# Experts in an order that interleaves the four groups, and the final norm formed inside each expert block

## The reference, cut to what matters

```python
g = jnp.argmax(gl, axis=-1)                       # one group for each token
top_v, top_i = lax.top_k(el_g, 2)                 # two experts inside it
gate = jax.nn.softmax(top_v, axis=-1) * p_g[:, None]
h_e = silu(x @ w_gate[e]) * (x @ w_up[e])         # x: the rows of hn sent to expert e
y = h + sum over the two experts of gate * (h_e @ w_down[e])
y_prompt, y_sample = rmsnorm(y, g_final)          # y / sqrt(mean(y*y) + 1e-6) * g_final
```

## Time and profile before

| | us |
|---|---|
| median of three runs | 2008.78 |
| profiled execution | 2014.13 |
| its span, first to last instruction | 2012.40 |
| TensorE busy in the span | 1877.3 (93%) |
| VectorE, ScalarE, GpSimd busy | 974.0, 773.4, 280.8 |

### The profile page before, as it was taken

The page is one execution under the profiler, slowest core; times in us unless marked ns, Lnnn a source line. Parts: engine busy times, 40 slices in busy tenths (PEclk is TensorE's granted clock), DMA queues, the critical chain, the costliest instruction groups (busy, mean ns, idle before and its releaser), DMA issues. The chain is left out here.

```text
span 2012.4 us, 28492 instructions
## 1 busy us (share of the span) xinstructions
PE 1877.3 (93%) x10232; PEld 1609.9 (80%) x10233; DVE 974.0 (48%) x1929; ACT 773.4 (38%) x1442; POOL 280.8 (14%) x387
## 2 busy tenths in 40 slices
PE   7899999999999999999999937999999999999980
PEld 5899987788888788887888736888888888888870
DVE  5634343546444654445454334445565554646424
ACT  4332323333333333333333204444465444636423
POOL 2000000000201001000010022222222222222223
PEclk9799999999999999999999958999999999999995
DMA  6222233423236222342232517655567566556438
GB/s 220 88 83 84 84 128 119 138 86 102 85 126 209 84 85 96 135 138 93 84 105 87 198 47 230 186 183 184 177 215 257 152 230 188 183 182 228 130 56 343
DMA packets 153429, 293.12 MB, mean 146 GB/s; under 512 B 9341, under 2 KB 75901, under 8 KB 153354
## 3 DMA queue, kind: packets, MB, share of 16 engines
q1 hardware_dynamic: 135930, 232.13, 32.9%
q0 software_dynamic: 15072, 51.45, 10.4%
q10 hardware_dynamic: 2352, 8.52, 1.0%
HBM read 243.02 MB, written 49.07 MB: 145 GB/s over the span
## 5 line engine op out<-in xcount | busy, mean ns | idle before, releaser
L62 PE MATMUL bank<-xT_hi,wh 128*128 128x512 f32 (+1 forms) x960 | 341.0, 355 | 7.2 <-ACT S L745 5.4
L63 PE MATMUL bank<-xT_lo,wh 128*128 128x512 f32 (+1 forms) x960 | 340.4, 355 | 0.0
L64 PE MATMUL bank<-xT_hi,wl 128*128 128x512 f32 (+1 forms) x960 | 339.2, 353 | 0.0
L793 DVE TENSOR_TENSOR wl<-raw,wh 128x512 fp32r<-128x512 f32 x352 | 219.4, 686 | 202.5 <-ACT wh L596 202.4
L1665 PE MATMUL bank<-gu_hi,ex_hi 128*128 128x256 f32 (+1 forms) x960 | 311.6, 325 | 4.6 <-DVE gu_lo L1575 4.6
L1667 PE MATMUL bank<-gu_hi,ex_lo 128*128 128x256 f32 (+1 forms) x960 | 307.3, 320 | 0.0
L1666 PE MATMUL bank<-gu_lo,ex_hi 128*128 128x256 f32 (+1 forms) x960 | 307.3, 320 | 0.0
L596 ACT ACTIVATE wh<-raw 128x512 fp32r<-128x512 f32 x352 | 192.0, 619 | 85.1 <-PE bank L1216 54.7
L62 PEld LDWEIGHTS bank<-xT_hi,wh 128*128 128x128 f32 x960 | 182.3, 190 | 35.9 <-issue 9.7
L1665 PEld LDWEIGHTS bank<-gu_hi,ex_hi 128*128 128x128 f32 x960 | 183.5, 191 | 24.7 <-DVE gu_lo L1575 8.2
L64 PEld LDWEIGHTS bank<-xT_hi,wl 128*128 128x128 f32 x960 | 182.4, 190 | 25.3
(11 more groups left out here) (228 smaller groups left out, 3154.8 us busy)
## 6 DMA issues: line engine op xcount, KB each, us to landing
raw<-in_w_in SPq DMA_DIRECT2D x56, 1024.0 KB, 5.2
raw_gate_up<-in_w_gate SPq DMA_DIRECT2D x16, 2048.0 KB, 8.4
raw_gate_up<-in_w_up SPq DMA_DIRECT2D x16, 2048.0 KB, 13.5
raw_d<-in_w_down SPq DMA_DIRECT2D x16, 2048.0 KB, 12.8
raw<-in_w_out SPq DMA_DIRECT2D x16, 1024.0 KB, 6.3
raw<-in_w_up_pool SPq DMA_DIRECT2D x16, 512.0 KB, 3.5
raw<-in_w_up_gmlp SPq DMA_DIRECT2D x16, 512.0 KB, 4.5
h<-in_x_prompt SPq DMA_DIRECT2D x16, 512.0 KB, 5.0
```

The costliest lines, as they stand in the source:

```text
L62: nc.tensor.matmul(out, lh, rh, start=(i == 0), stop=False)
L63: nc.tensor.matmul(out, lh, rl, start=False, stop=False)
L64: last = nc.tensor.matmul(out, ll, rh, start=False, stop=(i == n - 1))
L793: lo = lambda out, x, hi: tt(out, x, hi.bitcast(F32), ALU.subtract)
```

## The change

`phase_four` goes. Its work moves into the expert blocks. The experts are taken in the order (expert 0 of each of the four groups, then expert 1 of each, ...), so that two experts that can hold the same token never stand next to each other. Weights, slots and block numbers are looked up in that order by nested loops.

Each block now ends in `z`, the block's rows of `h` plus the weighted result. VectorE forms it (`add`, two instructions out of the PSUM banks, in place of ScalarE's `weigh`): at the start of the next block, or inside its weight split where that block is a first one. `z` is written to `h_rows` by a plain scatter. Its norm is formed at once: `square` on ScalarE, `mean` on VectorE, `root` on GpSimd, `scale` on VectorE as the last instruction of the block after the one that made the result. The normed rows are scattered to both outputs at every block: to the prompt output with out-of-range rows dropped, and to the sample output by a third index field that is out of range for every row that isn't a sample row. A token's rows are so written twice, and the later expert's value stays. The rows of `h` for a block are gathered a block ahead (`next_h`).

GpSimd's order for each block is now `step`:

```diff
-def fetch_and_add(col, j): ... gather x; wait y_out; wait y_read; scatter-add to h
+def step(col, j):
+    wait_apart(pool, x_tr, j, passed_pool)
+    nc.gpsimd.tensor_copy(idx_1[:, :], idx[:, :]).then_inc(moved, 1)
+    wait_apart(pool, moved, j, passed_pool)
+    rows_of_x(col, j)
+    store_z(j)
+    next_h(j + 1)
+    root(j)
+    store_final(j)
+    wait_apart(pool, z_out, 16 * j, passed_pool)
+    wait_apart(pool, prompt_out, 16 * j, passed_pool)
+    wait_apart(pool, sample_out, 16 * j, passed_pool)
```

```diff
+def store_final(n):
+    wait_apart(pool, final_ok, n + 1, passed_pool)
+    for to, field, last, landed in ((v["y_prompt"], 0, SEQ - 1, prompt_out),
+                                    (v["y_sample"], 2, SAMPLE - 1, sample_out)):
+        nc.gpsimd.indirect_dma_start(
+            out=to[0], in_=final[:, :], in_offset=None, bounds_check=last, oob_is_err=False,
+            out_offset=bass.IndirectOffsetOnAxis(ap=idx_y[:, field:field + 1], axis=0))\
+            .then_inc(landed, 16)
```

```diff
+def add(n):
+    dve.wait_ge(y_done, n)
+    dve.wait_ge(final_ok, n)
+    dve.wait_ge(h_rows_in, 16 * n)
+    for c in range(2):
+        stt(z[:, cols], bankY[c][:, :], idx_h[:, 1:2].bitcast(F32), h_rows[:, cols], ALU.mult, ALU.add).then_inc(z_ok, 1)
+def scale(n):
+    dve.wait_ge(z_rs, n)
+    dve.wait_ge(moved_y, n)
+    stt(final[:, :], z[:, :], rsz[:, 0:1], v["gf"][:, :], ALU.mult, ALU.mult).then_inc(final_ok, 1)
 def split(i, lo):
     for k in range(2 * KD):
+        if k == KD + 4:
+            add(lo + 1)
 def per_block(e, i, lo, j, first=False):
+    if not first:
+        add(j + 1)
+        mean(j + 1)
     ...
+    if first:
+        mean(j + 1)
     ...
+    scale(j + 1)
-def weigh(j): two ACTIVATE out of bankY
+def square(n):
+    act.wait_ge(z_ok, 2 * n)
+    nc.scalar.activation(sq[:, :], z[:, :], ACT.Square, accum_out=ssz[:, 0:1]).then_inc(z_ss, 1)
```

More of the change, by code:

```diff
@@ L46 @@
 NEG = -3.0e38
+FIELDS = 3
+NOWHERE = 1 << 20
 NPAN = 22
@@ L1032, in place @@
                     for c in range(2):
-                        nc.vector.tensor_copy(pay[0:r, c, span, 0:1].rearrange("p t o -> p (t o)"),
-                                              tok_all[0:r, column:column + span.stop - span.start])
+                        for field, table in ((0, tok_all), (2, sample_all)):
+                            nc.vector.tensor_copy(pay[0:r, c, span, field:field + 1].rearrange("p t o -> p (t o)"),
+                                                  table[0:r, column:column + span.stop - span.start])
                     nc.vector.tensor_copy(weight[:, 0, :], parts[0:r, 0, span])
@@ L1517, in rows_high, with split, per_block @@
                             .then_inc(ex_hi, 1)
[L1518 to L1528, removed]
+                rows_high(1)
+                def square(n):
+                    act.wait_ge(z_ok, 2 * n)
+                    nc.scalar.activation(sq[:, :], z[:, :], ACT.Square, accum_out=ssz[:, 0:1]).then_inc(z_ss, 1)
+                def split(i, lo):
                     use_sigmoid_table(1)
                     act.wait_ge(gu_done, lo + 1)
-                    act.wait_ge(gate_in, 16 * e + 16)
+                    act.wait_ge(gate_in, 16 * i + 16)
                     for k in range(1, 2 * KD):
                         if k == KD:
-                            act.wait_ge(up_in, 16 * e + 16)
-                        if k == KD + 6:
-                            weigh(lo)
+                            act.wait_ge(up_in, 16 * i + 16)
                         nc.scalar.activation(gu[0][:, k, :], raw_gu[:, k, :], ACT.Copy).then_inc(e_hi, 1)
-                def per_block(e, lo, j, first=False):
+                    square(lo + 1)
+                def per_block(e, i, lo, j, first=False):
                     def down(k):
@@ L1548, in per_block @@
                         use_sigmoid_table(0)
-                        weigh(j)
+                        square(j + 1)
                     act.wait_ge(g_done, j + 1)
@@ L1564, in per_block @@
                     if first:
-                        rows_high(j + 3, j)
+                        rows_high(j + 2)
                 experts(act, split, per_block, peel=True)
                 total = act.value_load(blk_tab[0:1, 2 * NE - 1:2 * NE], min_val=1, max_val=MAXBLK)
-                weigh(total)
+                square(total + 1)
             @block.vector
@@ L1647, in per_block @@
                         rows_low(2 * j + 3)
+                    scale(j + 1)
                 experts(dve, split, per_block, peel=True)
+                total = dve.value_load(blk_tab[0:1, 2 * NE - 1:2 * NE], min_val=1, max_val=MAXBLK)
+                add(total + 1)
+                mean(total + 1)
+                scale(total + 1)
             @block.tensor
```

269 lines of the change are left out of this document (123 added, 146 removed).

## The result

| | before | after | predicted |
|---|---|---|---|
| median, us | 2007.47 (2006.15 to 2011.86, 4 runs) | 2146.44 (2139.07 to 2151.68, 4 runs) | 2045 (2000 to 2110) |
| ratio to before | | 1.0685 [1.0652, 1.0718] | 1.018 |
| profiled execution, and its span | 2014.13, 2012.4 | 2151.68, 2149.8 | 2050.4 |

The direction was right, and the loss nearly four times too small. The time went to the expert blocks. First the windows of the changed kernel (stretch; us, PE, PEld, DVE, ACT, POOL busy, granted clock, DMA share, GB/s): the expert blocks, then a loop into a first block, the first 5 us behind it, and the rest of the loop out of that block.

A forecast was written before the change was run, and what follows sets the result against it. Bounds: TensorE's 18.35 us pace in the expert blocks, and the DMA-bound last stage. Loop losses of 84.7 us less gains of 48.4 gave +36.3, or 2050.4 profiled, carried to a median of 2045 us; range 2000 to 2110.

The forecast's parts named there:

- Into a first block: Loop from transposes to transposes ending at an expert's first block: 19.8 us against 18.1 before, late by 1.7, 15 times.
- scaling's end: VectorE's scaling of the normed rows ends 4.8 us after the transposes, or 8.0 after those of a first block.
- landing with the wake: Two stores of normed rows land in 4.9 us on idle DMA engines, 6.4 beside weight loads, before GpSimd goes on.
- from the copy to the gather's issue: On GpSimd after the stores land: wake, two index copies and the gather's issue, 1.7 us together.
- the gather: Fetch of the next block's x rows: 7.5 us into a first block, 5.2 out of one, 4.6 between others.
- this very rule: VectorE instructions with two SBUF inputs block GpSimd: up to 0.4 us per instruction, 30 us more, kept only in the range.
- Out of a first block: Loop starting at an expert's first block: 22.2 us against 18.5 before, late by 3.7, 16 times.
- Between others: Loops between blocks that are not first ones: 16.9 us, under the pace of 18.35, so no loss.
- The gains: Removed last stage saves 45.5 us and an earlier first gather 2.9 us, together 48.4.
- Dear stores: Rival: normed-row stores cost as much as the scatter-add, or the second costs like a full one; 2156 us; chance 0.22.
- Rows in time: Rival: x rows arrive in time and the last stage's gain stays; loss under 3.0 us per expert; 1993 us; chance 0.18.
- VectorE setting the pace: Rival: VectorE's added work in first blocks, not the rows, sets the pace; 52 us lost, 2013 us; chance 0.10.

The follow-up runs named there:

- the run without the hold: Changed kernel with VectorE's low-half split of gate and up weights reading PSUM and one SBUF tensor instead of two SBUF tensors; 2092.67 us, ratio 1.0427.
- the best version: Changed kernel with the gather of the next x rows behind the issue of the normed-row stores but ahead of the wait for their landing; 1984.12 us, ratio 0.9868.

## Why the prediction was wrong

**Into a first block** it failed, by 77 of the 99 us that the loops lost beyond the 84.7 predicted: 15 x (24.98 - 18.13) = 103 us in place of 25. Term by term, in the loop from 1270.26:

- scaling's end 4.72 (predicted 4.8), store's issue 0.91 (0.8), landing with the wake 4.49 (4.9): right;
- **from the copy to the gather's issue 4.79 (1.7 with the wake): the term that was mis-sized.** It was read off, from a place where VectorE was not splitting (the price beside a split stood in the same trace, below);
- the gather 10.71 (7.5): 2.2 of the 3.2 us are its own issue, held in the same way; the rest, 8.5, is 1.0 over the sum and a little over the end of 8.1 that it gave. Without the hold a gather took 8.29 (1327.14 to 1335.43).

Eleven of the 15 loops are like this, mean 26.3; in the four where the copy took 0.20 to 0.35 us the mean is 21.4. 11 x 4.9 = 54 us, about what the run without the hold won. I had weighed this very rule, put it at 0.4 us for each instruction and left it out of the sum, because the split would have gaps; the earlier trace rows shows its 16 instructions as one row of 9.86 us, with no idle time noted in it. The Trainium skill, "SBUF — State Buffer" (Who interferes with whom), says that a VectorE instruction with two SBUF inputs contends with a GpSimd instruction that reads SBUF, and the page's summary (Summary: rules for kernel authors) that the second to issue blocks until the first has finished. The runs agree on the pair and show more: the copy got no turn between twelve instructions set end to end.

That 0.4 us was too little could be read in the trace of before. In each of its 16 first blocks GpSimd's first two copies took about 1.27 and 0.97 us, beside VectorE's split of the down weights, as in the block of the 1.38 us that the prediction read:

```profile
1291.85 2.36 DVE L1575 TENSOR_TENSOR dn_lo<-raw_d,dn_hi 128x1024 fp32r<-128x1024 f32 x2
...
1291.86 1.27 POOL L1471 COPY idx<-idx 128x2 int32<-128x2 int32 x1 [2.77 <-PE bank L1657]
1293.29 0.97 POOL L1473 COPY idx<-idx 128x2 int32<-128x2 int32 x1 [0.16 <-POOL idx L1471]
```

**Out of a first block** 23.04 against 22.2: 73 us in place of 59. In the loop from 1295.88 the scaling ends 9.96 behind the transposes (8.0), because TensorE, having waited 6.41 us, was granted 0.50 of 2.4 GHz (1.2 GHz) in the next 5 us (with useless products in the wait it ended 7.7 behind); the sum took the durations of the earlier trace rows, made at a granted clock of 1.00. From the store to the copy 7.67 us (6.4): the landing was no dearer than forecast, but GpSimd passed to the next expert behind it, as in eight of these 16 loops. The gather took 4.35 (5.2).

**Between others** 19.06 in place of 18.01: 8.4 us, where nothing was predicted. Here it is the clock alone. TensorE waits for no rows at the end of these loops, but five of the eight begin behind a wait at a lower granted clock (0.66 over the first 5 us) and take 19.6 to 19.7 us; the three that begin at 1.00 take 18.0 to 18.1.

**The gains** came near: 46.4 us in place of 48.4, by two errors. The start gave 6.1 for 2.9; but the block table was also ready 3.6 us earlier, before the change acts, which leaves 2.5. The end gave 40.3 for 45.5. From the last product's end (2131.95 + 0.39 = 2132.34) to the span's end are 17.5 us, not 12.2:

```profile
2136.04 1.28 DVE L1695 SCALAR_TENSOR_TENSOR final_rows<-z_rows,rsz,gf 128x1024 f32<-128x1024 f32 x1 [0.79 <-POOL rsz L1521]
2138.21 1.04 POOL L1527 DMA_INDIRECT out<-final_rows,idx_y  x1 [2.21 <-DVE final_rows L1695]
2139.55 0.97 POOL L1527 DMA_INDIRECT out<-final_rows,idx_y  x1 [0.30 <-issue]
```

The stores go out 5.9 us behind the last product, earlier than worked out (7.3), and land after a median of 2.4 us in that stretch (4.9 in the sum). Then some 8 us follow in which the profile shows nothing; the sum had no such term.

**The rivals.** Dear stores: no, landings were as forecast, and the second store is free. Rows in time: no; the loops lost 183.8 by 16 = 11.5 us per expert, where 3.0 was its limit. VectorE setting the pace: not here, but it is what is left in the best version, where a loop into a first block is 0.9 longer than before, and VectorE forms the first `hid` 17.8 us behind the transposes and not 17.0; that rival put the add at 0.8. The three costs that I left out don't share a cause with any rival: each is a short instruction or a clock whose price changed with the place it was moved to.

## What to carry to other kernels

Price a small instruction in the stretch to which the change moves it, beside the engine that will be busy there, not where the old trace has it: a copy of 0.18 us became one of 2.9 to 3.4 us in 11 of 15 loops into a first block, and the run without that hold was 54 us faster. Behind a wait on an in-order queue everything is exposed, the loop's own bookkeeping too, so issue the next load ahead of the wait; that turned this change from 6.9% slower into 1.3% faster. And where a sum makes TensorE wait, its next stretch has to be priced at the lower clock as well.

## What the runs showed of the hardware that I had not expected

- GpSimd waited out a whole unbroken row of VectorE instructions with two SBUF inputs: a copy begun in the middle of twelve ended 3.40 us later, with the last of them, and an issue of an indirect DMA takes 3.17 us in place of 0.99. With one input from PSUM and one from SBUF both are back at 0.18 and 1.00 us.
- An indirect store whose rows are nearly all out of range adds nothing to the loop (1.0666 without it, 1.0685 with it, intervals overlapping).
- After a wait of 6.41 us TensorE was granted 0.50 for the next 5 us; with products in the wait 1.00.
- A program that ends with indirect stores on GpSimd's queue ended some 8 us behind their landing; before, with its last stores on ScalarE's queue, data moved until about 1 us ahead of the end.
